# A two-layer transformer kernel: two steps of layer A's hand-set order moved, and the loads of x issued from ScalarE

## The reference, cut to what matters

```python
for layer in range(DEPTH):                      # DEPTH = 2
    if layer < N_A_LAYERS:                      # layer A (0)
        qkv = (x @ a_w_qkv[layer]).reshape(B, S, 3, A_HEADS, A_HEAD_DIM)
        q = partial_rotary(qkv[:, :, 0], positions).transpose(0, 2, 1, 3)
        k = partial_rotary(qkv[:, :, 1], positions).transpose(0, 2, 1, 3)
        v = qkv[:, :, 2].transpose(0, 2, 1, 3)
        o = moba_attention(q, k, v).transpose(0, 2, 1, 3).reshape(B, S, D)
        x = layer_norm(DEEPNORM_ALPHA * x + o @ a_w_o[layer], ln_g[layer, 0], ln_b[layer, 0])
    else:                                       # layer B (1): differential attention, shared K/V
        ...
    f = conv_ffn(x, ffn_w_in[layer], ffn_conv_w[layer], ffn_conv_b[layer], ffn_w_out[layer])
    x = layer_norm(DEEPNORM_ALPHA * x + f, ln_g[layer, 1], ln_b[layer, 1])
```

## Time and profile before

| what | value |
| --- | --- |
| median of 3 runs | 589.12 us (588.91 to 589.55) |
| the profiled execution: its time | 589.41 us |
| the profiled execution: its span, first to last instruction | 587.6 us |
| TensorE busy | 577.4 us (98%) |
| VectorE busy | 449.9 us (77%) |
| ScalarE busy | 332.7 us (57%) |
| GpSimd busy | 50.5 us (9%) |

### The profile page before, as it was taken

How to read it: one execution, slowest core, us unless ns; L and a number is a source line. 1 busy time by engine, 2 the same in 40 slices (tenths; PEclk the granted TensorE clock), 3 DMA queues, 4 the chain that set the end, 5 groups by cost and what they waited for, 6 DMA issues and landing times.

```text
span 587.6 us, 7718 instructions
## 1 busy us (share of the span) xinstructions
PE 577.4 (98%) x2701; PEld 471.3 (80%) x2701; DVE 449.9 (77%) x818; ACT 332.7 (57%) x557; POOL 50.5 (9%) x84
## 2 busy tenths in 40 slices
PE   8999999999999999999999999999999999999995
PEld 6877877888888888888888888888888888888883
DVE  4889997976788776767879796778677887766656
ACT  5766664246566565455545678945455564555530
POOL 5300000400000000000220003132000000000003
PEclk9999999999999999999999999999999999999999
DMA  8997877466768897766367965342955889877511
GB/s 298 304 341 225 266 232 207 148 199 198 234 205 296 282 313 245 231 227 207 122 214 235 293 186 173 117 144 77 314 182 178 253 264 324 255 238 241 180 36 72
DMA packets 96242, 128.65 MB, mean 219 GB/s; under 512 B 13468, under 2 KB 74188, under 8 KB 96204
## 3 DMA queue, kind: packets, MB, share of 16 engines
q1 hardware_dynamic: 94764, 123.97, 66.2%
q0 software_dynamic: 1152, 4.19, 2.0%
q10 hardware_dynamic: 288, 0.00, 0.0%
HBM read 108.23 MB, written 1.05 MB: 186 GB/s over the span
## 4 chain that ended last, share of the span: by engine, by line
PE 89%; DVE 3%; DMA 3%; POOL 2%; issue 1%; ACT 1%; SPq 0%; DVEq 0%; ACTq 0%
PE wide L1327 16%; PE wide L1329 15%; PE wide L1328 15%; PE score L1329 6%; PE score L1327 6%; PE score L1328 6%; PE outb L1329 3%; PE outb L1327 3%; PE turn L1327 3%; PE turn L1329 3%; PE turn L1328 3%; PE outb L1328 3%; DMA raw<-in_a_w_qkv 1%; DVE w_lo L1009 1%; DMA spare<-turned 1%
## 5 line engine op out<-in xcount | busy, mean ns | idle before, releaser
L1009 DVE TENSOR_TENSOR w_lo<-raw,w_hi 128x2048 fp32r<-128x2048 f32 (+1 forms) x120 | 210.5, 1776 | 58.5 <-ACT w_hi L806 58.1
L806 ACT ACTIVATE w_hi<-raw 128x2048 fp32r<-128x2048 f32 (+1 forms) x126 | 184.1, 1488 | 97.2 <-PE wide L1329 47.1
L1327 PE MATMUL wide<-w_hi,oT_hi 128*128 128x512 f32 x240 | 94.8, 395 | 0.0
L1329 PE MATMUL wide<-w_hi,oT_lo 128*128 128x512 f32 x240 | 93.5, 390 | 0.0
L1328 PE MATMUL wide<-w_lo,oT_hi 128*128 128x512 f32 x240 | 93.5, 390 | 0.0
L1327 PE MATMUL wide<-w_hi,xT 128*128 128x512 f32 x220 | 88.1, 401 | 0.6 <-ACT qk_rows L870 0.6
L1329 PE MATMUL wide<-w_hi,xT 128*128 128x512 f32 x220 | 85.9, 390 | 0.0
L1328 PE MATMUL wide<-w_lo,xT 128*128 128x512 f32 x220 | 85.8, 390 | 0.0
L1327 PE MATMUL score<-w_hi,xT 128*128 128x512 f32 x160 | 62.3, 389 | 0.0
L1328 PE MATMUL score<-w_lo,xT 128*128 128x512 f32 x160 | 62.3, 389 | 0.0
L1329 PE MATMUL score<-w_hi,xT 128*128 128x512 f32 x160 | 62.3, 389 | 0.0
(11 more groups left out here) (168 smaller groups left out, 836.6 us busy)
## 6 DMA issues: line engine op xcount, KB each, us to landing
raw<-in_ffn_w_in SPq DMA_DIRECT2D x88, 512.0 KB, 5.3
raw<-in_ffn_w_out SPq DMA_DIRECT2D x22, 1024.0 KB, 7.7
kT<-turned SPq DMA_DIRECT2D x104, 128.0 KB, 2.8
raw<-in_a_w_qkv SPq DMA_DIRECT2D x9, 1024.0 KB, 5.8
raw<-in_w_kv_shared SPq DMA_DIRECT2D x8, 1024.0 KB, 5.6
raw<-in_a_w_o SPq DMA_DIRECT2D x4, 1024.0 KB, 6.3
raw<-in_b_w_q SPq DMA_DIRECT2D x4, 1024.0 KB, 5.2
raw<-in_b_w_o SPq DMA_DIRECT2D x4, 1024.0 KB, 5.0
```

Source lines behind the costliest of these rows:

```text
L806: ins = nc.scalar.activation(w_hi[c % RING][:, part], raw[c % RAW_RING][:, part], ACT.Copy)
L1009: ins = nc.vector.tensor_tensor(w_lo[c % RING][:, part], raw[c % RAW_RING][:, part], w_hi[c % RING][:, part].bitcast(F32), ALU.subtract)
L1327: nc.tensor.matmul(dst, a_hi, b_hi, start=start, stop=False, skip_group_check=True)
L1329: return nc.tensor.matmul(dst, a_lo, b_hi, start=False, stop=stop, skip_group_check=True)
```

## The change

It has two parts. In `mixer_schedule` a new function `place` takes a step out of an engine's list and puts it in ahead of (0) or behind (1) another one, four times, for layer A alone. And the four loads of x are issued by ScalarE ahead of its loads of the positions, so that SyncE's first instructions are loads of weights. Nothing is computed in another way.

```diff
+    def place(engine, step, at, behind):
+        order[engine].remove(step)
+        order[engine].insert(order[engine].index(at) + behind, step)
+
+    if A:
+        place("ACT", ("drain", 2, 0), ("split_hi", first_chunk + 8, 0), 0)
+        place("ACT", ("out_hi", 0), ("exp", 12), 1)
+        place("DVE", ("out_lo", 0), ("prob_turn", 11), 1)
+        place("DVE", ("out_lo", 1), ("mask", 15), 1)
...
         def _(sp):
-            def load_x(f):
-                st, half = divmod(f, 2)
-                cols = slice(half * HALF, (half + 1) * HALF)
-                sp.dma_start(xs[:, st, cols], x[0, st * P:(st + 1) * P, cols]).then_inc(x_in[f], 16)
...
-            load_x(0)
...
                                 sp.dma_start(raw[c][:, q * HALF:(q + 1) * HALF],
                                              src[:, q, :]).then_inc(piece_in[q] if q < PIECES - 1 else raw_in[c], 16)
-                                if q == 0:
-                                    load_x(X_ORDER[1])
-                            load_x(X_ORDER[2])
-                            load_x(X_ORDER[3])
...
         def _(act):
+            for f in X_ORDER:
+                st, half = divmod(f, 2)
+                cols = slice(half * HALF, (half + 1) * HALF)
+                act.dma_start(xs[:, st, cols], x[0, st * P:(st + 1) * P, cols]).then_inc(x_in[f], 16)
             for st in range(ST):
                 act.dma_start(pos_i[:, st:st + 1], positions[0, st * P:(st + 1) * P].rearrange("(p o) -> p o", o=1)
                               ).then_inc(pos_in, 16)
```

## The result

The changed kernel takes 595.42 us (median of 6 runs, 594.57 to 596.29) against 589.12: ratio 1.0105, 95% interval 1.0096 to 1.0115. It is slower, by 6.3 us where 3.8 was forecast, and 0.9 above the top of the range. Its profiled execution took 595.45, of which 593.3 is the span.

The account below looks back on a forecast made before the run. It took the thread from the positions through GpSimd and VectorE to `pv(3)` as the bound behind a barely full TensorE. Late positions +4.3 and attention -0.47 gave +3.8 on 589.12, so 592.9 us, range 590.2 to 594.5.

Parts of the forecast that it names:

- What bounds: Layer A: TensorE only just full; the thread behind it runs from the positions through GpSimd and VectorE to `pv(3)` at 97.51.
- d: Delay of GpSimd's angles, hence of `split_lo(3)`, from positions landing at 10.6 instead of 5.3: 4.3 us, bounds 1.6 to 5.9.
- the terms at nothing: Stretches forecast at 0: `split_lo(3)` to `prob_turn(7)`, `prob_turn(15)` to `pv(3)`, and outside the span.
- The drain at nothing: `drain(2, 0)` ahead of `split_hi(8)` runs in ScalarE's idle time; TensorE saves 0.73, VectorE gets nothing, so 0 in the sum.
- The clock: Rival: TensorE's clock falls in its wait for chunk 3, mostly hidden, up to 2 us more: 594.9; chance 8%.
- TensorE's wait: At chunk 3's first product: 0.8 us of cover, so TensorE waits d - 0.8, here 3.5 us.
- this start hardly matters: Start of TensorE's own products: a shift between -0.3 and +1 us vanishes in the wait for chunk 3.
- The attention steps: Moved exp, turn and mask order fills VectorE's gap ahead of `out_lo(0)`: -0.47 us, bounds 0 and -0.98.
- The wait at `pv(3)`: TensorE's wait there for the last probabilities would be about 2 us, longer than before.
- only the issue counts: Rival: the positions are put off by issue time alone, landing at 7.1; +1.1, 590.2 us; chance 10%.
- the positions come sooner: Rival: the positions land sooner than before and both TensorE waits go, 0.73 + 0.75: 587.6 us; chance 4%.
- VectorE catches up: Rival: chunk 8 lands quicker, so 1.3 us of VectorE's wait for it come back: 591.6 us; chance 13%.

Follow-up runs that it names:

- pos_late: Kernel before, x still on SyncE's queue, with ScalarE issuing the two loads of the positions behind its first copies of x: 596.57 us, ratio 1.0119.
- only_order: Kernel before with the four moved steps alone, x loaded as before: 588.55 us, ratio 0.9994.
- drain_only: Kernel before with only the drain moved ahead of ScalarE's split of chunk 8: 589.14 us, ratio 0.9995.
- fill: Changed kernel plus 12 matmuls of zeros, result unread, on TensorE ahead of its wait for chunk 3: 593.87 us, ratio 1.0074.
- only_x: Changed kernel without the four moved steps, so only x's loads moved to ScalarE ahead of the positions: 595.48 us, ratio 1.0114.
- pos_first: Changed kernel with ScalarE issuing the loads of the positions first and x's four behind them: 592.5 us, ratio 1.0061.
- drain_back: Changed kernel with the drain put back behind ScalarE's split of chunk 8: 595.62 us, ratio 1.0109.
- angles_behind: Changed kernel with ScalarE's sines and VectorE's cosine and sine tables taken behind their splits of chunk 3: 593.01 us, ratio 1.0069.
- x_last: Kernel before with only the fourth quarter of x issued by ScalarE, behind the positions: 589.88 us, ratio 1.0013.

## Why the prediction was off

- **What bounds: right up to `split_lo(3)`, incomplete behind it.** The chain from the positions through GpSimd to `split_lo(3)` was the one that counted; `pos_late` moved it alone, and the end moved with it. But "From there VectorE sets the pace" left out that ScalarE's splits, and VectorE behind them, wait for TensorE at the ring of four and, in the new order, at the drain's bank. From `pv(3)` on all is shifted alike: 490.08 against 490.09 us.
- **The step that failed: the size of d.** "Behind x landing at 9.1 I take 1.5 more: 10.6", then "a delay of d = 4.3". Measured: x's last quarter lands at 9.6, the positions 1.8 behind it, at 11.4 (+0.8 in all). GpSimd's chain from `pos_f` to the angles took 12.8 us instead of the 12.5 reckoned (+0.3). And I had rounded the result down from 4.5, "a little less for a later overlap", for which no row spoke (+0.2). With the 4.3 these add up to 5.6, and the measured d is 5.67. It lies within the bounds that I had given (5.9), but the likeliest value stood too far down in them. With 5.67 for d the same sum gives 594.3, still inside the range, whose ends moved d alone; the terms at nothing, next, took the time out of it. That x would land "some 0.6" earlier without the 4-byte packets between was the first wrong half-microsecond: it landed when it had before.
- **The drain at nothing: the second step that failed, +0.19 net by luck.** I put it into ScalarE's idle time, "ends at 38.4". The bank is full at 38.05 to 38.5 with positions in time (`only_order`, `drain_only`) and at 44.6 with late ones, so the drain costs VectorE 0.1, 0.7 and 0.9; and "VectorE [...] gets nothing" was wrong as well: 0.69 come back by `prob_turn(7)`, through the ring.
- **The clock: priced as a rival at 8%, and it happened.** The halved clock came behind the idle of 2.49 us, from 30 to 33. I had it hidden by TensorE's slack of 1.9 us at `pv(3)`. There TensorE still had to wait; what I missed is a place on its way where others wait for TensorE, the drain's bank. `fill` puts its cost at 1.5 us by the medians. The Trainium skill's page "TensorE: Matmul & The Clock Gate" (Part 1, the HAM clock gate) says that the clock is halved after idling; by this the trace agrees.
- **TensorE's wait: 2.6 us instead of 3.5**, since its own products started at 12.70, 2.3 late, where I had allowed 1. That this start hardly matters held as far as the wait for chunk 3 covers it: `only_x` starts at 11.93 and takes the same time. In `pos_first`, where the positions are in time and nothing covers it, a start 3.2 late goes with a loss of 3.5.
- **The attention steps: right.** -0.44 against -0.47, and no idle ahead of `out_lo(0)`.
- **The wait at `pv(3)`: wrong sight.** 1.15 from start to start instead of a longer one of about 2; by `fill`, where TensorE gets there 1.8 sooner, the slack went into the slow clock. That the last transfer landed 0.3 later is within what unlike kernels show (6.5 to 7.4 from `prob_turn(15)` to `pv(3)`), so no part of the change need be behind it.
- **Outside the span: not thought of.** +0.31, see below.
- **Rivals.** That only the issue counts is refuted by the landing times, and that the positions come sooner by the same. That VectorE catches up can't be seen in the changed kernel; in `fill`, with the clock kept, VectorE does take 1.2 us less from `split_lo(3)` to `prob_turn(7)` than before, 0.7 of it the drain's.

## What to carry to other kernels

Before a load is put on another queue, list what that queue already carries and follow the smallest of it: 1 KB of positions at the head of ScalarE's queue was the start of the path that counted. Where a step waits in a bound queue, ask not only when its input is ready in the trace before, but what it holds up once that input is late. Do so for the engine that seems full as well: TensorE was, and still ScalarE and VectorE waited for it at two places. And of a delay with no cover, the likeliest value is that of the transfer's own rows, not one rounded towards no change.

## What the runs showed of the hardware beyond that

A tiny transfer on an idle queue was not served at once while another queue had much outstanding. In `pos_late` the positions were issued at 4.85 and 5.27 to a queue that held nothing else. They took 5.9 and 7.0 us to land, against 2.9 and 4.1 as the first of the program. The queues from 5.3 to 8.5 us in `pos_late`, in the same columns as above; this is the only one that moved a packet:

```profile
q1 hardware_dynamic: 548, 1.00, 95.3%
```

So where both queues have a backlog the packets alternate, but here the newcomer's first packet came only behind 8.5, at least 3.6 us after its issue. In the kernel before the positions had none before 2.0 and 44 from 2.0 to 2.5, so the first came 1.3 to 1.8 us after the issue at 0.73. The Trainium skill's page "DMA: Bandwidth & Descriptors" (section "Queues, rings and completion order") has each engine serve its queues by turns, packet by packet; by this alone the positions would have passed SyncE's backlog, and the trace of `pos_late` doesn't show that. The measurement decides; why is open.

Time outside the span was 2.12 to 2.15 us in every profiled execution with all of x on ScalarE's queue (the changed kernel, `only_x`, `pos_first`, `drain_back`, `fill`, `angles_behind`) and 1.79 to 1.83 in the eight others, the kernel before among them. It is 0.3 of the 6.3. `x_last`, with one quarter of x on that queue, is among the eight, so one such transfer isn't enough; no trace shows what it is.

An operation of 128x16 elements on GpSimd takes 0.22 to 0.26 us with VectorE idle and mostly 0.5 to 0.6, now and then up to 1.1, beside VectorE's splits. The angles' chain, 12.8 us in the changed kernel, takes 14.6 in `angles_behind`, where it also runs beside `split_lo(3)`; two of its operations there take 1.06 and 1.10.

Not tried: the two columns of positions on two queues with one semaphore.
